# The mean of squares behind a projection's first chunk, at four places of a two-layer decoder step

## What is computed

```python
def rmsnorm(x, g):
    y = x * lax.rsqrt(jnp.mean(x * x, axis=-1, keepdims=True) + EPS)
    return y * g

def hybrid_layer(h, ...):
    z = rmsnorm(h, g_mix) @ w_in            # then three token mixers -> y
    h = h + y @ w_o
    h = h + ffn(rmsnorm(h, g_ffn))          # layer 0: dense SwiGLU, layer 1: top-2 of 8 experts
    h = h + sigmoid(rmsnorm(h, g_ple) @ w_ple_gate) * (p_i @ w_ple_proj)
```

## Time and profile before

| | |
|---|---|
| three executions | 1173.37, 1174.75, 1175.77 us, median 1174.75 |
| the profiled execution | 1174.76 us, of which its span is 1173.0 us |
| mean granted TensorE clock | 0.958 of full |
| TensorE busy | 1086.3 us (93%) |
| VectorE busy | 945.0 us (81%) |
| ScalarE busy | 716.9 us (61%) |
| GpSimd busy | 89.9 us (8%) |

### The profile page before, as it was taken

The page is one execution under the profiler, slowest core; times in us unless marked ns, Lnnn a source line. Parts: engine busy times, 40 slices in busy tenths (PEclk is TensorE's granted clock), DMA queues, the critical chain, the costliest instruction groups (busy, mean ns, idle before and its releaser), DMA issues.

```text
span 1173.0 us, 17576 instructions
## 1 busy us (share of the span) xinstructions
PE 1086.3 (93%) x6380; PEld 962.7 (82%) x6380; DVE 945.0 (81%) x1278; ACT 716.9 (61%) x871; POOL 89.9 (8%) x119
## 2 busy tenths in 40 slices
PE   6996999999998997867999999999999999999485
PEld 6995999999997996866888888888888888888365
DVE  6998766566777899655989989899999989999565
ACT  5435444444444433535888888888888887788442
POOL 5420000000002330000000000000000000000200
PEclk9998999999999999977999999999999999999768
DMA  8422445535433342314999999999999999999600
GB/s 337 171 87 74 154 184 206 215 144 210 158 137 144 145 148 84 116 65 157 379 356 402 360 379 376 355 405 363 391 361 374 393 348 412 355 387 378 242 2 37
DMA packets 24309, 293.07 MB, mean 250 GB/s; under 512 B 3144, under 2 KB 3176, under 8 KB 7360
## 3 DMA queue, kind: packets, MB, share of 16 engines
q1 hardware_dynamic: 20464, 279.24, 62.2%
q0 software_dynamic: 3792, 13.11, 2.9%
HBM read 285.03 MB, written 7.31 MB: 249 GB/s over the span
## 4 chain that ended last, share of the span: by engine, by line
PE 77%; DVE 17%; issue 2%; DMA 2%; ACT 2%; POOL 0%; DVEq 0%; ACTq 0%; POOLq 0%; SPq 0%
PE bank L557 15%; PE bank L561 15%; PE bank L560 15%; PE bank L598 9%; PE bank L601 8%; PE bank L602 8%; DVE wlo L1111 4%; DVE cv L1185 4%; DVE rstd L1123 2%; PE bank L613 2%; PE bank L519 1%; PE bank L503 1%; PE bank L473 1%; PE bank L509 1%; DMA ring<-y_rows,row_id 1%
## 5 line engine op out<-in xcount | busy, mean ns | idle before, releaser
L1040 DVE TENSOR_TENSOR wlo<-ring,whi 128x1024 fp32r<-128x1024 f32 x384 | 461.5, 1222 | 48.5 <-ACT whi L730 38.5
L730 ACT ACTIVATE whi<-ring 128x1024 fp32r<-128x1024 f32 x384 | 404.9, 1060 | 86.7 <-PE bank L557 80.7
L557 PE MATMUL bank<-whi,gh_hi 128*128 128x512 f32 x512 | 205.0, 400 | 0.6 <-DVE gh_lo L1046 0.6
L561 PE MATMUL bank<-whi,gh_lo 128*128 128x512 f32 x512 | 201.2, 393 | 0.0
L560 PE MATMUL bank<-wlo,gh_hi 128*128 128x512 f32 x512 | 200.4, 391 | 0.0
L791 ACT ACTIVATE whi<-ring 128x1024 fp32r<-128x1024 f32 x137 | 143.4, 1051 | 77.4 <-PE bank L598 74.3
L598 PE MATMUL bank<-hid_hi,whi 128*128 128x264 f32 x608 | 180.5, 297 | 8.5 <-ACT pp L802 5.4
L602 PE MATMUL bank<-hid_hi,wlo 128*128 128x264 f32 x608 | 175.2, 288 | 0.0
L601 PE MATMUL bank<-hid_lo,whi 128*128 128x264 f32 x608 | 175.1, 288 | 0.0
L1111 DVE TENSOR_TENSOR wlo<-ring,whi 128x1024 fp32r<-128x1024 f32 x137 | 166.3, 1225 | 0.6
L598 PE MATMUL bank<-gh_hi,whi 128*128 128x264 f32 x480 | 137.8, 287 | 1.4 <-DVE wlo L1111 1.3
(11 more groups left out here) (195 smaller groups left out, 1370.1 us busy)
## 6 DMA issues: line engine op xcount, KB each, us to landing
ring<-wstream SPq DMA_DIRECT2D x131, 2048.0 KB, 8.3
y_rows<-work POOLq DMA_DIRECT2D x8, 512.0 KB, 8.4
h<-x_in SPq DMA_DIRECT2D x1, 1056.0 KB, 4.9
y_out<-work POOLq DMA_DIRECT2D x2, 528.0 KB, 3.0
xn_rows<-work SPq DMA_DIRECT2D x2, 512.0 KB
par<-par_in SPq DMA_DIRECT2D x2, 494.5 KB, 7.0
c_sample<-xc POOLq DMA_DIRECT2D x2, 372.0 KB, 3.7
stc<-state_in SPq DMA_DIRECT2D x2, 360.0 KB, 9.2
```

What stands on the lines that cost most here:

```text
L557: mm = pe.matmul(out[:, :], xh, whi[:, pos, cols_], start=(k == 0), stop=False)
L561: mm = pe.matmul(out[:, :], xl, whi[:, pos, cols_], start=False, stop=(k == last))
L730: nc.scalar.activation(whi[:, q % SPLITS, :], quarter_at(q), ACT.Copy).then_inc(S["hi"], 1)
L1040: v.tensor_tensor(wlo[:, q % SPLITS, :], quarter_at(q), whi[:, q % SPLITS, :].bitcast(F32), ALU.subtract).then_inc(S["lo"], 1)
```

## The change

At A to D TensorE's program has the first chunk of the next projection ahead of the average; the other chunks follow behind it. At the first norm of layer 0, ahead of the experts in layer 1, and at the last norm the order is as before. So that the first ple chunk of layer 1 (chunk 138, bank 2) may be written while DVE still adds the turned sums to h, block k of the sums now lies in bank (k + 138) % 8, which puts block 0 into bank 2.

```diff
-                average(bank[4], D_MODEL, [sq[:, k, :] for k in range(KD)], S["ms"], (S["sq_mix"], 1))
-                project(B["zc"], N_ZC, *mix, S["gh_mix"])
+                if l == 0:
+                    average(bank[4], D_MODEL, [sq[:, k, :] for k in range(KD)], S["ms"], (S["sq_mix"], 1))
+                project(B["zc"], 1, *mix, S["gh_mix"])
+                if l:
+                    average(bank[4], D_MODEL, [sq[:, k, :] for k in range(KD)], S["ms"], (S["sq_mix"], 1))
+                project(B["zc"] + 1, N_ZC - 1, *mix)
...
-                average(bank[4], D_MODEL, [sq[:, k, :] for k in range(KD)], S["ms"], (S["sq_ffn"], 1))
                 if l == 0:
...
-                    project(B["ff"], KF, *ghs, S["gh_ffn"])
+                    project(B["ff"], 1, *ghs, S["gh_ffn"])
+                    average(bank[4], D_MODEL, [sq[:, k, :] for k in range(KD)], S["ms"], (S["sq_ffn"], 1))
+                    project(B["ff"] + 1, KF - 1, *ghs)
...
                 else:
+                    average(bank[4], D_MODEL, [sq[:, k, :] for k in range(KD)], S["ms"], (S["sq_ffn"], 1))
                     route(pe)
...
-                            mm = pe.transpose(bank[(k + 4) % KD][:, j * P:j * P + TOKS[j]],
+                            mm = pe.transpose(bank[(k + BASE[1]["ple"]) % KD][:, j * P:j * P + TOKS[j]],
...
+                project(B["ple"], 1, *ghs, S["gh_ple"], tail if l else dense)
                 average(bank[4], D_MODEL, [sq[:, k, :] for k in range(KD)], S["ms"], (S["sq_ple"], 1))
-                project(B["ple"], KD, *ghs, S["gh_ple"], tail if l else dense)
+                project(B["ple"] + 1, KD - 1, *ghs, S=tail if l else dense)
...
-                        link(nc.vector.tensor_tensor(h[:, k, :], h[:, k, :], bank[(k + 4) % KD][:, 0:T], ALU.add))
+                        link(nc.vector.tensor_tensor(h[:, k, :], h[:, k, :], bank[(k + BASE[1]["ple"]) % KD][:, 0:T], ALU.add))
```

## The result

The changed kernel takes 1180.01 us, the median of nine runs (1177.1 to 1182.19), against 1175.29 us for the kernel before in nine runs beside it (1173.37 to 1176.7). The ratio is 1.004, 95% interval 1.0027 to 1.0052: it is 4.7 us slower, with 3.2 to 6.1 us as the interval. The forecast of 1177.6 us had the sign; the time lies 0.6 us above the range of 1175.2 to 1179.4 us.

A forecast was written before the change was run, and what follows sets the result against it. The prediction read the last chain as 77% TensorE and 17% VectorE, with VectorE pacing layer 0's ple stage. It summed 0 + 2.3 + 0.3 + 0.2 = 2.8 us onto 1174.76 us: 1177.6 us, range 1175.2 to 1179.4 us.

The forecast's parts named there:

- A: From wo to ff: VectorE's spare time takes up a first evacuation 2.3 us late; 0 us, bounds 0 and 0.3.
- B: Layer 0, down2 to ple: VectorE is the pace, so the late root costs +2.3 us, bounds 2.2 to 2.5.
- C: Layer 0's ple to layer 1's zc: late sigmoid makes TensorE wait; +0.3 us, bounds -0.1 and +1.5.
- D: Layer 1, experts to ple: first evacuation 2.4 us late, nearly all given back; +0.2 us, bounds -0.1 and +0.6.
- TensorE's part: At C: start 0.51 us earlier, 0.41 us more work behind it, so the second chunk ends -0.10 us.
- the surcharge for half clock: At C and D: 1.9 us extra for TensorE at half clock, left the same in the changed order.
- the rival's 1.6: Clock stays up: C -1.6, D about -1.7 us, 1173.8 us in all; chance 0.08 both places, 0.12 one.
- the prediction's own sign: Wrong if C's or D's clock reads full at the last operand, or layer 0's ple evacuations wait for TensorE.
- its other signs: A's third evacuation level; B's evacuations 3.80 us apart; C's sigmoid directly behind its table load; D's last evacuations not awaiting TensorE.
- The queue at C: Rival at C: ACT's copies and table loads delay the low part more; C +1.5 us, 1178.9 us; chance 0.14.
- Nothing: Rival: all four places covered, or B's delay absorbed by a wait ending elsewhere; 1174.8 us, chance 0.06.

The follow-up runs named there:

- after_again: The changed kernel unedited, run again with a profile of another execution: 1181.36 us, ratio 1.0047 to the kernel before; the profiled execution took 1182.55 us.
- only_B: The kernel before with only the move at B (layer 0, down2 to ple): 1177.45 us against 1174.83 us, ratio 1.002.
- B_half: The kernel before with, at B alone, the average behind four of the first chunk's eight groups: single time 1178.3 us.
- C_pool_later: only_C with GpSimd's diagonals held back until layer 1's second gated product is made: one execution, 1176.42 us against 1174.82 us before.
- only_D: The kernel before with only the move at D and the sums' banks renumbered: 1176.31 us against 1174.83 us, ratio 1.0015.
- only_C: The kernel before with only the move at C (layer 1's zc): 1175.42 us against 1174.83 us, ratio 1.0008.
- C_one_copy: only_C with one of ACT's two copies of weights put behind the sigmoid: one execution, 1173.78 us against 1174.82 us before.
- D_again: only_D unedited, run once more for another execution's clock: 31.80 us from the last add to the last reciprocal.
- D_filled: only_D with six unused matmuls behind the first chunk's groups 1 to 6 and other sum banks: 1174.69 us against 1174.26 us before, ratio 1.0004.
- inter_D2: The kernel before with chunk groups and average matmuls by turns at D alone: 1172.35 us against 1175.11 us, ratio 0.9977.
- inter_CD2: The kernel before with chunk groups and average matmuls by turns at C and D: 1167.42 us against 1175.11 us, ratio 0.9941.
- best: inter_CD2 with one weight copy ahead of C's first sigmoid and GpSimd's diagonals behind the second gated product: 1167.47 us, ratio 0.9945 to the kernel before.

## Why the prediction was right and where it was not

**A, right.** 12.29 us against 12.26; in after_again 12.27. VectorE's spare 0.86 us an evacuation took the delay up within two chunks.

**B, right in size and mechanism.** 2.3 us were forecast and 2.3 measured, in three profiles; only_B is 2.4 us by its ratio. With the average in the middle of the chunk (B_half) the delay was the 0.85 us that the same sum gives. The new waits of TensorE for low parts, 2.7 to 5.7 us, are mostly here (five of 0.65 us, where before had two), and cost nothing: VectorE paces this stage, and TensorE only meets that pace sooner.

**C, too small: 0.3 us forecast, 1.0 measured at equal clock.** The mechanism held. The sigmoid was forecast 0.55 us late and came 383.09 - 370.70 = 12.39 us behind the eighth evacuation against 11.84: 0.55. The step that failed is the sum around it. TensorE's part was written -0.1 us and was +0.25 (11.43 against 11.18 us to the third chunk). The low part was given 0.14 us of slack behind an on-time multiply and on-time copies of VectorE; with GpSimd beside them these took 0.4 us more (0.65 against 0.43 us, 2.53 against 2.35), and TensorE waited 0.53. GpSimd's diagonals had been dismissed as covered by 11 us, which looked only at who needs their result, not at whom they run beside; C_pool_later, which holds them back, gives the 0.4 us back to TensorE's fourth chunk. The bounds, to +1.5, hold the value.

**D, too small as well: 0.2 us forecast, 0.5 measured at equal clock, 1.8 by the ratio of only_D (0.7 to 2.8).** The working from the profiled execution was near: first evacuation 2.4 us late forecast, 2.74 in only_D; most of it given back by the idleness in front of the evacuations at the end; 0.46 us left (32.22 against 31.76, with full clock 5.8 and 5.7 us behind the last add; 32.05 in after against 31.57 in B_half, at 5.4 and 5.3 us). The term that was short is the first evacuation's delay, by 0.3 us; the forecast had carried the surcharge for half clock over unchanged from the old order.

What the forecast left out is that the clock's rise is not at the same place in each execution. In six profiles with the old order at D the clock returned to full 5.3 to 5.9 us behind the last add in three, and 2.9 to 3.0 us behind it in the other three, where D took 30.5 us and not 31.6 to 31.9 (only_C, C_pool_later and C_one_copy, all with the old D). In the four with the changed order it came after 4.9 to 5.8 us. The means are 31.1 and 32.0 us: 0.9 us, if the sample is taken as it is. But the four don't show that the change loses the early rise. The half clock that ends here begins behind the experts' last matmul, and its length doesn't tell the orders apart: 30.7 us in five of the six old profiles and in only_D and D_again, 34.1 us in before, after and after_again. Windows of before, and below them one of only_C:

```profile
1101.10:1135.20 34.10, 17.44 (x53) 11.19 (x54) 15.16 (x28) 10.51 (x15) 6.10 (x7) 0.50 0.23 79
1135.30:1136.30 1.00, 1.00 (x10) 1.00 (x10) 0.00 (x0) 0.09 (x1) 0.00 (x0) 1.00 0.00 0
```

```profile
1105.10:1135.70 30.60, 14.67 (x41) 8.42 (x42) 13.36 (x27) 7.82 (x12) 6.09 (x7) 0.50 0.25 88
```

The rise came early in the three profiles in which the half clock had begun 27.7 to 27.8 us ahead of the last add. In the other three of the old order it had begun 24.8, 25.5 and 28.4 us ahead, in the four of the changed order 24.9 to 25.8 and 28.7 us: none of these lies where the early rises were seen. So where the half clock happened to begin would account for the two groups without the change, and whether the changed order would rise early from there isn't shown.

What TensorE did before the rise differs: in the old order one average matmul of 0.84 us in each 1.25 us between operands, in the changed one a group of three at 0.66 us (the forecast had 0.72). With either the clock rose only behind the last add, in all ten profiles. With six matmuls put into the gaps (D_filled), or by turns (inter_D2, inter_CD2, best), it was full 0.9 to 3.3 us ahead of the last add, in four of four: that filling the gaps brings the rise forward is shown. The Trainium skill, "TensorE: Matmul & The Clock Gate", section "Why this matters for your kernels", says to leave no idle gaps between matmul bursts. It speaks of longer gaps than the 0.2 us that the rows list in front of each group here; these experiments agree with it for short ones too, and the change itself left gaps as large as those it meant to fill.

**The rivals.** The full clock at C came in the one profile and brought 1.7 us against half clock, about the rival's 1.6; the kernel was slower even so. By the prediction's own sign, a full clock at C when the last operand comes, it was wrong there; its other signs, at A, B and D and the sigmoid at C, came as written. Whether the change brings the full clock at C isn't shown: the changed order was seen with 0, 3.4 and 6.8 us at half (one, three and one profiles), the old one with 3.4 and 6.8 (five and two). The queue at C was the right rival and reached 1.0 of its 1.5 us. "Nothing" fell.

**The step that failed, in one place.** The sum was 1.9 us short of the 4.7 measured. Of this 0.7 us is C, where 0.3 stood for what measured 1.0: TensorE's part had the wrong sign, and GpSimd's diagonals beside VectorE were put at nothing. Another 0.3 us is D at equal clock. The remaining 0.9 us has no place that the runs show.

**What stays open.** By stages at equal clock the change costs 2.3 + 1.0 + 0.5 = 3.8 us, by the timed runs 4.7 (3.2 to 6.1): the rest is within the interval, but only_D, D_filled and inter_D2 were each some 1 us or more slower by their ratios than their stage at D says (1.8 against 0.9 us; +0.5 against -1.0; -2.7 against -3.6, the stage each time against the mean of 31.1 us; only for D_filled is that outside the interval), and why isn't shown. The new bank numbers of the sums, which were never changed alone, are hardly the reason: from the first transpose into them to the last add it is 13.8 to 14.8 us in the six profiles with the old numbers and 14.1 to 14.9 in the four with the changed order's. The stretch from the mixers to the last sum, of which the change touches only these numbers, took 706.8 to 710.5 us over all fourteen profiles, of changed and unchanged kernels alike (710.18 in inter_D2, 706.77 in C_one_copy); whether the changed kernel meets the longer ones more often isn't shown.

## What to carry to other kernels

Before work is put in front of a statistic to fill a gap, ask what covers the statistic's tail (here root and reciprocal, 2.75 us) afterwards; if the next instruction that needs it belongs to the pacing engine, the tail is the price, less what that engine had to spare. Doing both by turns, the statistic one block behind, fills the gap and keeps the cover: at C and D alone 6.9 us faster (5.3 to 8.5), where the plain move at all four places was 4.7 us slower. Ask also what else starts behind a late result, and beside whom it then runs. And where the clock rises or falls at a place, one profile is a sample: compare stages between profiles with equal clock, and look at when the half clock began before a difference in its end is put down to the change.

## What the runs showed of the hardware

- The same kernel at the same place spent 0 and 6.8 us at half clock in two executions (C, after and after_again), worth 2.6 us there (51.08 and 53.70 us).
- Half clock in front of D ended ahead of the last add only where TensorE's gaps between operands were filled (D_filled and the three kernels by turns, four of four profiles; none of ten otherwise).
- GpSimd's twelve diagonals of 128x128 took 7.73 us before, 8.81 us in only_C and 10.80 us in C_pool_later. The difference is whole instructions: one diagonal takes 0.60 us, but the one that meets VectorE's two low parts takes 2.38 us (2.48 for one in C_pool_later) and ends 0.39 us behind them (387.12 against 386.73 us in only_C). Before, none met them; in only_C one did, in C_pool_later two. The Trainium skill, "GPSIMD Engine Reference", section "8. Key points", names contention with VectorE instructions that read two operands from SBUF; GpSimd's rows agree. On VectorE's side the rows are mixed: the multiply took 0.65 us beside it in only_C but 0.43 us in C_one_copy, with GpSimd running there too.
- A table load again had no tail: in only_C 381.80 + 1.28 = 383.08 us, and the sigmoid starts at 383.09. The 1.38 us of draining that the Trainium skill, "ScalarE: Activation LUTs", section "What ACT_TABLE_LOAD costs", gives were seen in no run: of the 28 table loads in each profile, every one whose next instruction didn't wait for another engine was followed by it within 0.1 us.
